# Who adds up the squares of the edge norms: TensorE tile by tile, in the place of GpSimd's adds

## What is computed

```python
def rms_norm(x, g, eps=NORM_EPS):
    xf = x.astype(jnp.float32)
    y = xf * lax.rsqrt(jnp.mean(xf * xf, axis=-1, keepdims=True) + eps)
    return (y * g.astype(jnp.float32)).astype(x.dtype)
...
        h = rms_norm(x, sandwich_g[i, 0]) * (1 + sc_m) + sh_m
...
        x = x + gt_m * rms_norm(y, sandwich_g[i, 1])
        h = rms_norm(x, sandwich_g[i, 2]) * (1 + sc_f) + sh_f
        y = jnp.square(jax.nn.relu(h @ ffn_w1[i])) @ ffn_w2[i]
        x = x + gt_f * rms_norm(y, sandwich_g[i, 3])
```

## Time and profile before

| what | value |
|---|---|
| runs | 1650.17, 1652.42, 1655.12 us; median 1652.42 |
| profiled execution | 1650.32 us, its span 1648.5 us |
| TensorE busy | 1530.8 us, 93% of the span |
| TensorE weight loads | 1266.4 us, 77% |
| VectorE, ScalarE busy | 877.1 us (53%), 526.0 us (32%) |
| GpSimd busy | 115.7 us, 7% |
| of it the adds of squares (L389) | 33 of 1.51 us in the mean between sq buffers, and 9 more of 1.53 to 1.54 |
| mean granted clock of TensorE | 0.943 |

### The profile page before, as it was taken

One profiled execution on the slowest core, in us unless ns is written; L12 is line 12 of the kernel. 1 busy time (PEld: TensorE's weight loads), 2 busy tenths in 40 slices (PEclk: granted clock), 3 DMA queues, 4 the chain that ended last, 5 costly groups with the idle time before them and its releaser, 6 DMA issues. The chain is left out here.

```text
span 1648.5 us, 19330 instructions
## 1 busy us (share of the span) xinstructions
PE 1530.8 (93%) x7679; PEld 1266.4 (77%) x7679; DVE 877.1 (53%) x1361; ACT 526.0 (32%) x678; POOL 115.7 (7%) x105
## 2 busy tenths in 40 slices
PE   7988999959999999967999999979995999999997
PEld 7767566748888888855888999978874888888885
DVE  5768365687676676545566444432426534333433
ACT  4423223343131322234756200102334413231331
POOL 0000000230000000032112100000213000000000
PEclk9989699969999999987999999999996999999997
DMA  8535002505655556312221111030221233223221
GB/s 280 165 101 167 31 1 68 185 26 184 201 169 189 181 175 192 115 53 95 59 78 52 39 33 39 8 102 27 78 77 51 77 102 103 84 94 102 84 70 52
DMA packets 159596, 164.35 MB, mean 100 GB/s; under 512 B 9486, under 2 KB 155164, under 8 KB 159260
## 3 DMA queue, kind: packets, MB, share of 16 engines
q1 hardware_dynamic: 159516, 163.25, 31.2%
HBM read 157.20 MB, written 6.03 MB: 99 GB/s over the span
## 5 line engine op out<-in xcount | busy, mean ns | idle before, releaser
L150 DVE TENSOR_TENSOR w_lo<-w_raw,w_hi 128x2048 fp32r<-128x2048 f32 (+1 forms) x97 | 221.2, 2281 | 111.0 <-ACT w_hi L145 110.8
L145 ACT ACTIVATE w_hi<-w_raw 128x2048 fp32r<-128x2048 f32 (+1 forms) x97 | 182.1, 1877 | 254.8 <-PE bank L157 242.9
L155 PE MATMUL bank<-h_hi_mlp,w_lo 128*128 128x512 f32 x512 | 204.6, 400 | 6.2 <-DVE h_lo_mlp L357 6.2
L155 PE MATMUL bank<-mlp_u_hi,w_lo 128*128 128x512 f32 x512 | 204.5, 399 | 0.0
L157 PE MATMUL bank<-h_hi_mlp,w_hi 128*128 128x512 f32 x512 | 203.0, 396 | 0.0
L156 PE MATMUL bank<-h_lo_mlp,w_hi 128*128 128x512 f32 x512 | 202.4, 395 | 0.0
L156 PE MATMUL bank<-mlp_u_lo,w_hi 128*128 128x512 f32 x512 | 201.8, 394 | 0.0
L157 PE MATMUL bank<-mlp_u_hi,w_hi 128*128 128x512 f32 x512 | 201.5, 394 | 0.0
L278 DVE SCALAR_TENSOR_TENSOR ada_acc<-ada_raw,c_act,ada_acc 128x256 f32<-128x256 f32 x280 | 137.6, 491 | 10.0
L155 PE MATMUL bank<-h_hi_gdn,w_lo 128*128 128x512 f32 x320 | 138.2, 432 | 2.5 <-DVE kt L1701 2.5
L156 PE MATMUL bank<-h_lo_gdn,w_hi 128*128 128x512 f32 x320 | 128.4, 401 | 0.0
(11 more groups left out here) (289 smaller groups left out, 2385.2 us busy)
## 6 DMA issues: line engine op xcount, KB each, us to landing
w_raw<-in_ffn_w SPq DMA_DIRECT2D x64, 1024.0 KB, 5.6
ada_raw<-in_ada_w SPq DMA_DIRECT2D x44, 1024.0 KB, 5.3
w_raw<-in_gdn_w_in SPq DMA_DIRECT2D x16, 1024.0 KB, 5.8
w_raw<-in_mla_w_o SPq DMA_DIRECT2D x4, 1024.0 KB, 6.5
w_raw<-in_gdn_w_o SPq DMA_DIRECT2D x4, 1024.0 KB, 4.9
y<-in_x SPq DMA_DIRECT2D x1, 2048.0 KB, 8.1
v_tok<-in_ada_w SPq DMA_DIRECT2D x2, 1024.0 KB, 12.7
y<-in_ada_w SPq DMA_DIRECT2D x2, 1024.0 KB, 7.1
```

Source lines behind the costliest of these rows:

```text
L145: act.activation(w_hi[n % 2][:, 0:size[n]], w_raw[n % 2][:, 0:size[n]], ACT.Copy).then_inc(w_hi_ready, 1)
L150: dve.tensor_tensor(w_lo[n % 2][:, 0:size[n]], w_raw[n % 2][:, 0:size[n]], w_hi[n % 2][:, 0:size[n]].bitcast(F32), ALU.subtract).then_inc( ...
L155: pe.matmul(ps, s_lo, m_hi, start=first, stop=False)
```

## The change

TensorE sums every squared tile by itself, with `sum_tile`, and GpSimd adds none.

- y norm: `square_y` alternates between sq[0] and sq[1] and waits for the sum of the tile two before. In the out-projections TensorE sums tile t-1 after it has made tile t; where the first two tiles are made in one pass (delta rule), it sums tile 0 right behind them. In the last group of an MLP it sums tile t-9 after result tile t. Tile 7 is summed in the edge.
- x norm: the eight squares go to sq[0] and sq[1] in turn, and TensorE sums each.
- GpSimd: the adds go. Its clearing of y waits for the last read of y in the edge instead.

```diff
         def square_y(act, b, t, src):
 
             if t >= 2:
-                act.wait_ge(sem("edge_y_added"), ADDS * b + t - 1)
-            act.activation(sq[min(t, 1)][:], src, ACT.Square).then_inc(sem("edge_y_squared"), 1)
...
+                act.wait_ge(sem("edge_y_summed"), KD * b + t - 1)
+            act.activation(sq[t % 2][:], src, ACT.Square).then_inc(sem("edge_y_squared"), 1)
 
         def edge_pe(pe, b, nxt):
-            sum_added(pe, "edge_y", b, sum_bank)
+            sum_tile(pe, KD - 1, KD, "edge_y", b, sum_bank)
             spread(pe, "edge_y", b)
             if nxt:
-                sum_added(pe, "edge_x", b, mod_bank)
+                sum_tiles(pe, KD, "edge_x", b, mod_bank)
                 spread(pe, "edge_x", b, mod_bank)
...
                 for k in range(KD):
                     act.wait_ge(x_new, KD * b + k + 1)
-                    if k >= 3:
-                        act.wait_ge(sem("edge_x_added"), ADDS * b + k - 2)
-                    slot = sq[0] if k == 0 else (sq[1], hf[0])[(k - 1) % 2]
-                    act.activation(slot[:], x[:, k], ACT.Square).then_inc(sem("edge_x_squared"), 1)
-                root_of_mean(act, 1, "edge_x", 1 / D, b, mod_bank)
+                    if k >= 2:
+                        act.wait_ge(sem("edge_x_summed"), KD * b + k - 1)
+                    act.activation(sq[k % 2][:], x[:, k], ACT.Square).then_inc(sem("edge_x_squared"), 1)
+                root_of_mean(act, KD, "edge_x", 1 / D, b, mod_bank)
...
                                 if k == KD - 1:
                                     last.then_inc(tile_done, 1)
+                        sum_tile(pe, 0, KD, "edge_y", edge, sum_bank)
...
                         last.then_inc(tile_done, 1)
+                        if t:
+                            sum_tile(pe, t - 1, KD, "edge_y", edge, sum_bank)
                         for m in ada_at[n - n0 - 1] if i == 0 and n > n0 else ():
...
-            def op_pool(pool):
-                add_squares(pool, "edge_y", edge, (sq[1],))
...
                                 last.then_inc(tile_done, 1)
+                                if final and t > KD:
+                                    sum_tile(pe, t - KD - 1, KD, "edge_y", edge + 1, sum_bank)
...
-                    edge_pool(pool, edge, usq)
-
+                    pool.wait_ge(yr_ready, KD * (edge + 1))
                     for i in range(2):
                         pool.memset(y[:, 4 * i:4 * i + 4], 0.0).then_inc(y_added, 1)
-                    add_squares(pool, "edge_y", edge + 1, (sq[1],))
```

More of the change, by code:

```diff
@@ L370, in build @@
         yr_ready, x_new, factors_ready = sem("yr_ready"), sem("x_new"), sem("factors_ready")
-        ADDS = KD - 2
         def square_y(act, b, t, src):
             if t >= 2:
-                act.wait_ge(sem("edge_y_added"), ADDS * b + t - 1)
-            act.activation(sq[min(t, 1)][:], src, ACT.Square).then_inc(sem("edge_y_squared"), 1)
[L383 to L403, removed]
+                act.wait_ge(sem("edge_y_summed"), KD * b + t - 1)
+            act.activation(sq[t % 2][:], src, ACT.Square).then_inc(sem("edge_y_squared"), 1)
         def edge_pe(pe, b, nxt):
-            sum_added(pe, "edge_y", b, sum_bank)
+            sum_tile(pe, KD - 1, KD, "edge_y", b, sum_bank)
             spread(pe, "edge_y", b)
             if nxt:
-                sum_added(pe, "edge_x", b, mod_bank)
+                sum_tiles(pe, KD, "edge_x", b, mod_bank)
                 spread(pe, "edge_x", b, mod_bank)
-        def edge_pool(pool, b, hf):
-            add_squares(pool, "edge_x", b, (sq[1], hf[0]))
         def edge_act(act, b, nxt, hf, xr, h_hi, n_round=None, beside=None):
-            root_of_mean(act, 1, "edge_y", 1 / D, b)
+            root_of_mean(act, KD, "edge_y", 1 / D, b)
             if nxt:
@@ L975, in op_dve @@
                         ada_finish(dve, m)
-            return op_sp, op_pe, op_pool, op_act, op_dve
+            return op_sp, op_pe, op_act, op_dve
         def out_projection(name, n0, s_hi, s_lo, ada_at, edge):
-            op_sp, op_pe, op_pool, op_act, op_dve = out_projection_parts(name, n0, s_hi, s_lo, ada_at, edge)
+            op_sp, op_pe, op_act, op_dve = out_projection_parts(name, n0, s_hi, s_lo, ada_at, edge)
             with nc.Block() as block:
@@ L988, in _ @@
                     op_pe(pe)
-                @block.gpsimd
-                def _(pool):
-                    op_pool(pool)
                 @block.scalar
@@ L1222, in gdn @@
             n0, tile0 = N_GDN, tiles_to[N_GDN]
-            op_sp, op_pe, op_pool, op_act, op_dve = out_projection_parts(
+            op_sp, op_pe, op_act, op_dve = out_projection_parts(
                 "gdn_o", N_GWO, o_hi, o_lo, [[]] * 4, 2, on_rest)
@@ L1536, in _ @@
                 def _(pool):
-                    edge_pool(pool, 1, hf)
                     for h in range(HEADS):
```

## The result

The changed kernel takes 1660.5 us (median of 6 runs, 1655.4 to 1664.3), the kernel before 1650.3 beside it (6 runs, 1646.1 to 1655.1): ratio 1.0056, 95% interval [1.0034, 1.0078], or 5.6 to 12.9 us slower. In another job it was 1659.4 (11 runs) against 1651.9 (34 runs), ratio 1.0054 [1.0035, 1.0074]. It is slower, as forecast, by 9.2 and 8.9 us by the two ratios (10.2 and 7.6 by the medians) where I had reckoned 16.1. Its profiled execution took 1655.42 us.

What follows compares the result with a forecast made beforehand. TensorE was taken to bound the touched stages, so added sums are paid in full: +25.1 in the products, -4.8 in y norm tails, -4.2 in x norms, +16.1 us on 1652.42, giving 1668.5. Range 1655 to 1675.

Steps and rivals of the forecast that it cites:

- What bounds the kernel, and the price of one sum: In the out-projections and MLPs TensorE is busy nearly always, so each added sum costs 0.90 us in full.
- How many are paid: Seven sums between products in each of four edges, 28 in all; one nearly free in layer 0's out-projection, -0.9 us.
- The second ada reduction: Only the first stage's last ada reduction was said to wait for VectorE, 0.7 us; no other was counted.
- The stall in the delta rule's out-projection: In layer 1's out-projection, tile 0's sum waits for its square after the interleaved pass: +0.8 us.
- The tails of the y norm: After the last product one tile is summed instead of two, the following steps unchanged: -4.8 us over four edges.
- The x norm: In three edges TensorE sums eight tiles at 1.707 us each and becomes the bound: 1.4 us saved each, -4.2.
- The sum: Products +25.1, y norm tails -4.8, x norms -4.2: +16.1 us in all.
- The base: The +16.1 us was added to the profiled 1650.32 us and to the three-run median 1652.42, giving 1666.4 and 1668.5.
- The range: 1655 to 1675 us overall, from the forecast's own 1663 to 1674 plus the case of two edges at high clock.
- rival B: TensorE's clock is up in one or two edges alone, 6.7 us less each: 1661.8 or 1655.1; chance 0.12.
- Rival A: The sums keep TensorE's clock up in three edges, 6.7 us less each: 1648.4, not slower; chance 0.10.
- Rival C: Squares come late and stall the in-stream sums among the products, up to 18 us: 1687; chance 0.05.

Runs made afterwards that it cites:

- The late sum of tile 6: Changed kernel with tile 6 of y summed in the edge, right before tile 7, not behind the last product: 1662.5 us, ratio 1.006.
- the warmed one: Changed kernel plus throwaway 512-column products around the spreads and between the x norm's sums in edges 0 to 2: 1658.6 us, 0.8 under the changed kernel.
- The filler: The hybrid plus seven throwaway 512-column products behind the x norm's spread in edges 0 to 2: 1631.9 us, ratio to before 0.9881.
- the hybrid: Against before: GpSimd still adds y squares, TensorE sums the running sum behind the last product; x norm as changed. 1637.8 us (0.9898), again 1637.4 (0.9919).
- the y norm's half: Against before, only the y norm changed, GpSimd still adding for the x norm: 1666.4 us, ratio 1.0082.
- the delayed one: Kernel before plus six extra ScalarE squares ahead of the x norm's root in edge 0, a pure delay: 1652.8 us, ratio 1.0009.
- the x norm's half: Against before, only the x norm changed, y norm left with GpSimd's adds: 1642.1 us, ratio 0.9932; again 1646.3 us, ratio 0.996.

## Why the forecast was right in direction and 6 us too high

- **What bounds the kernel, and the price of one sum: right.** Sums were paid in full, at 0.89 against 0.90.
- **How many are paid: this step failed.** "In each of the four edges seven tiles are summed between the products, 28 in all": the seventh stands behind the last product, in the wait for tile 7, and I saw its cover in the first out-projection only, in the last reduction's wait for VectorE (that -0.9 came true). 24 are paid: 2.7 us too much. The late sum of tile 6 and the two distances of 2.09 show it.
- **The second ada reduction: overlooked.** "The one place where one does" was wrong: an earlier reduction of the same stage waited 0.7 us for VectorE too, and paid for nearly half of the sixth sum, 0.4.
- **The stall in the delta rule's out-projection:** 0.25, not 0.8. The two tiles don't "end together, at about 1202.07": the last step of the pass starts at 1202.54 in that trace, and tile 0's square, at 1202.27, runs while the pass is still ending. Half a microsecond.
- **The tails of the y norm: undersized.** The forecast had -4.8, with "the root, inverse and spread behind it ... unchanged". From the first profile of before to the first of the changed kernel the tails shrank by 4.0, since the spreads of edges 2 and 3 lost the high clock (1.16 to 2.03, 1.18 to 2.08). But that one profile of before was a good case there: in two later ones these spreads took 2.07 already and the sums up to 2.99. Between the means of all profiles the tails shrank by 6.3. The forecast should have taken the low clock's price in edges 2 and 3 as well.
- **The x norm: right.** -4.2 forecast; 14.5 us from the first square to the last sum in every profile that has it but the warmed one, TensorE as the bound, VectorE's tiles 1.38 apart.
- **The sum.** 25.1 forecast for the products, 20.6 by the stages' means (21.2 reckoned; the two MLPs grew by 4.6 each and not by the 5.3 of six sums, the out-projection of layer 0 had the dip in one of two profiles); -9.0 forecast for the edges, -10.5 found. Together +10.1, and the two comparisons have +9.2 and +8.9 by their ratios.
- **The base.** One profile and a median of three runs were taken for a kernel whose runs spread over 13 us. Three more runs of it took its median from 1652.4 to 1650.3, so the forecast time of 1668.5 is 8 us too high where the difference is 6.
- **The range: luck.** 1660.5 lies inside 1655 to 1675, but below the forecast's own 1663 to 1674 (and the bounds that it names add up to 1665.9 to 1675.5). The lower part of the range was there for rival B, which did not occur; the measured time got there by the three unpaid sums, the smaller stall, the tails and the lower base.
- **Rival A** did not occur: 0.50 with TensorE at 100%. By the Trainium skill ("TensorE: Matmul & The Clock Gate", "Part 1: The HAM clock gate (the "warmup" mystery)") activity releases the throttle. The filler agrees (0.93 and 1.00 for 0.50 and 0.64). The gapless sums of the x norm speak against it: with no other products among them they took 13.8 us at 0.50, in every profile that has them. **Rival B** did not occur either: all three x norms took 13.8 us. **Rival C** neither: no in-stream sum but that of tile 0 waited for a square.

**Left open.** Why the delta-rule stretch takes 433.5 to 433.8 us in both profiles of the hybrid and in the y norm's half, about 438 in every one of before (the delayed one too) and of the x norm's half, and either in the changed kernel. Most of the difference lies in two short dips of the granted clock (0.69 and 0.66 for 1.00, above), so 4 us of the hybrid's gain may hang on when it meets these places; no run here tells what decides it.

## What to carry to other kernels

Before moving work onto the engine that bounds a stage, count which instances land in a wait that is there anyway: those are free, the others cost their full step; here one sum of seven was free. By the stages, moving only that one (the hybrid, against the x norm alone) took off 4.1 us, and moving all seven (the changed kernel, against the same) added 15.5. Fill a wait ahead of a long stretch of products with products of the same shape: seven of them in 3.1 us of idle time, in three edges, brought 5.6 us by the medians and 4.8 by the stages. And where an unchanged stage moves by 4 us between executions, compare stage by stage over several profiles before believing a difference of a few microseconds.

## What was not expected of the hardware

- Sums of one column in f32, back to back for 13.8 us, leave the granted clock at 0.50; when products had raised it first, it fell back to 0.50 with TensorE 100% busy. Behind seven single-pass products of 512 columns (344.74 to 347.42) the granted clock was 0.93 in the mean of 346 to 350, where the hybrid without them had 0.50.
- VectorE's update of x takes 0.68 us beside GpSimd's clearing of y (338.70 to 342.25) as alone. Beside GpSimd's adds of squares, in edge 0 of the kernel before, it took 0.98 from the fourth tile on (334.95), and the tiles came 1.68 apart in the place of 1.38.
- A table load of ScalarE of 1.28 us in edge 0 lay hidden behind TensorE's sums and became the last to end once these took 1.02.
